# A gated-delta stage on one NeuronCore: recalled values through the chunk's inverse, decays by transposes, 512-wide outer products, another order at the first and last chunk

## What is computed

```python
L = where(strict, einsum(kb, ki) * decay, 0)          # kb = ki * beta
rhs = concat([vi * beta, kb * exp(gi)])
u, wk = split(triangular_solve(L + eye, rhs))
v_new = u - wk @ S
o = (qi * exp(gi)) @ S + attn @ v_new
S = S * exp(g_last) + (ki * exp(g_last - gi)).T @ v_new
```

## Time and profile before

| what | value |
|---|---|
| median of 3 runs | 1588.41 us (1588.24 to 1590.96) |
| the profiled execution's own time | 1588.98 us |
| its span, first to last instruction | 1587.2 us |
| PE / DVE / ACT / POOL busy share of the span | 93% / 57% / 41% / 13% |
| mean granted PE clock | 0.951 |

### The profile page before, as it was taken

One profiled execution on the slowest core, in us unless ns is written; L12 is line 12 of the kernel. 1 busy time (PEld: TensorE's weight loads), 2 busy tenths in 40 slices (PEclk: granted clock), 3 DMA queues, 4 the chain that ended last, 5 costly groups with the idle time before them and its releaser, 6 DMA issues. The chain is left out here.

```text
span 1587.2 us, 31920 instructions
## 1 busy us (share of the span) xinstructions
PE 1479.2 (93%) x13294; PEld 1320.5 (83%) x13294; DVE 900.5 (57%) x1197; ACT 648.6 (41%) x1108; POOL 208.7 (13%) x217
## 2 busy tenths in 40 slices
PE   6999989899889999999999998879879999999994
PEld 6999978889889999999999997458867777777773
DVE  5676534755465443444444754543366777676776
ACT  5343534442143222222232413552434565665661
POOL 0111024554011000000011100220011000000002
PEclk8999999999889999999999997889879999999997
DMA  6678240000352323231334530005137888888886
GB/s 177 226 267 280 78 120 2 2 2 3 107 156 72 106 79 106 79 103 57 91 91 131 151 103 21 1 1 134 72 121 240 287 289 294 290 295 268 272 284 239
DMA packets 169741, 226.13 MB, mean 142 GB/s; under 512 B 11272, under 2 KB 134689, under 8 KB 169545
## 3 DMA queue, kind: packets, MB, share of 16 engines
q1 hardware_dynamic: 160246, 191.44, 38.7%
q0 software_dynamic: 8512, 30.48, 5.3%
q10 hardware_dynamic: 862, 2.50, 0.4%
HBM read 188.78 MB, written 37.88 MB: 143 GB/s over the span
## 5 line engine op out<-in xcount | busy, mean ns | idle before, releaser
L276 DVE TENSOR_TENSOR w_lo<-w_raw,w_hi 128x2048 fp32r<-128x2048 f32 (+1 forms) x71 | 153.9, 2172 | 91.4 <-ACT w_hi L268 91.4
L268 ACT ACTIVATE w_hi<-w_raw 128x2048 fp32r<-128x2048 f32 (+1 forms) x71 | 128.1, 1810 | 124.0 <-PE P L221 118.5
L221 PE MATMUL P<-xf_hi,w_hi 128*128 128x260 f32 x704 | 141.8, 282 | 2.0 <-DVEq L1764 1.2
L221 PE MATMUL P<-xf_hi,w_lo 128*128 128x260 f32 x704 | 141.9, 283 | 0.0
L221 PE MATMUL P<-xf_lo,w_hi 128*128 128x260 f32 x704 | 141.7, 283 | 0.0
L221 PEld LDWEIGHTS P<-xf_hi,w_hi 128*128 128x128 f32 x704 | 108.5, 188 | 2.6 <-issue 1.4
L221 PEld LDWEIGHTS P<-xf_hi,w_lo 128*128 128x128 f32 x704 | 108.5, 188 | 0.0
L221 PEld LDWEIGHTS P<-xf_lo,w_hi 128*128 128x128 f32 x704 | 108.2, 188 | 0.0
L221 PE MATMUL P<-xa_hi,w_hi 128*128 128x260 f32 x512 | 104.1, 285 | 2.7 <-DVE xa_lo L319 2.7
L221 PE MATMUL P<-xa_hi,w_lo 128*128 128x260 f32 x512 | 104.1, 285 | 0.0
L221 PE MATMUL P<-xa_lo,w_hi 128*128 128x260 f32 x512 | 103.9, 285 | 0.0
(11 more groups left out here) (553 smaller groups left out, 3320.5 us busy)
## 6 DMA issues: line engine op xcount, KB each, us to landing
raw_more_moe<-in_moe_w_gu_dram SPq DMA_DIRECT2D x64, 512.0 KB, 5.3
w_raw<-in_moe_w_gu_dram SPq DMA_DIRECT2D x64, 512.0 KB, 5.4
w_raw<-in_dense_w_gu_dram SPq DMA_DIRECT2D x44, 512.0 KB, 4.5
expert_out<-zeros POOLq DMA_DIRECT2D x40, 512.0 KB, 4.1
w_raw<-in_a_w_in_dram SPq DMA_DIRECT2D x32, 512.0 KB, 5.0
raw_more_moe<-in_moe_w_down_dram SPq DMA_DIRECT2D x32, 512.0 KB, 4.8
w_raw<-in_moe_w_down_dram SPq DMA_DIRECT2D x32, 512.0 KB, 4.7
w_raw<-in_dense_w_down_dram SPq DMA_DIRECT2D x16, 384.0 KB, 4.0
```

The lines of the kernel that those rows point to most:

```text
L221: ins = nc.tensor.matmul(out[:, b], w, x[:, b * HALF:(b + 1) * HALF], start=(first and n == 0), stop=(last and n == 2))
L268: ins = nc.scalar.activation(hi, raw, ACT.Copy)
L276: ins = nc.vector.tensor_tensor(lo, raw, hi.bitcast(F32), ALU.subtract)
```

## The change

- **Recall.** POOL decays the keys in place (`decay_keys`), `recall` multiplies them with the state directly (before the inverse is joined), DVE subtracts the product from the values (`less_recalled`), and one `solve` puts the difference through the inverse. `weigh_F`, `solve_keys`, the negated copy and the exponentials `e_tok` go.
- **Decays** are spread by transposes of a broadcast column, not by matmuls.
- **Key norms.** `factors` on DVE adds epsilon to the sums itself, and no longer waits for ACT's square root.
- **Sample outer products** are 512 wide, 2 for each step and not 8: the deltas are masked (`mask_deltas`) and the keys kept (`k_keep`). They start at level 8 of the last chunk, where `sample_back` has moved ahead of `level_two`.
- **First chunk.** `values`, `query_sums` and the second chunk's `decay` move behind its level 2; the exponential table is loaded at the phase's start; three of six copies of edge rows go to DVE.
- **POOL** scales the diagonal blocks first and the corner blocks (`scale_corner`) after the pieces.
- **Last chunk.** Its output gathers in bank 1 (`last_from_state` before the solve); its squares are one ACT instruction for each group, summed by DVE; the prompt's last `add_state` on DVE stands behind the gate.
- **Weights of the output projection.** The first chunk's high part (ACT) and low part (POOL, `EarlyWeights`), four of eight high parts of the activations and the first low part are made at the end of the delta phase. For this the buffers lie otherwise: the inverse's own where the weight chunk will be.

The diff, cut to its core and with 8 columns of indentation less inside functions:

```diff
-        LTc, LT12, cc = big("LTc", g), big("LT12", g, n), small("c", g, n)
-        nc.gpsimd.tensor_tensor(LTc, LTc, per_head(cc, 64), ALU.mult)
-        prep[g].done(nc.gpsimd.tensor_tensor(LT12[upper], LT12[upper], per_head(cc[upper], 64), ALU.mult), "pool", n, "LT")
+        LTc = big("LTc", g)
+        prep[g].done(nc.gpsimd.tensor_tensor(LTc, LTc, per_head(small("c", g, n), 64), ALU.mult), "pool", n, "LT")
...
+    def scale_corner(g, n):
+        LT12 = big("LT12", g, n)
+        ins = nc.gpsimd.tensor_tensor(LT12[upper], LT12[upper], per_head(small("c", g, n)[upper], 64), ALU.mult)
...
+    def decay_keys(g, n):
+        prep[g].after(pool, n, pe="qk", act="e_row")
+        prep[g].done(nc.gpsimd.tensor_tensor(tokens(1, g, n), tokens(1, g, n), big("ER", g), ALU.mult), "pool", n, "k_dec")
...
-            chain[g].after(pool, n - 1, pe="Wk", pool="FE")
+            inv[g].after(pool, n - 1, pe="Y32")
...
-    def weigh_F(g, n):
...
+        nc.gpsimd.tensor_tensor(d_mask[:, k], prod[:, k].unsqueeze(1).broadcast_to([128, TS, 128]),
                                 cols(c, CPLACE, TS).unsqueeze(2).broadcast_to([128, TS, 128]), ALU.mult).then_inc(s_masked, 1)
...
+            if last and s in (2, 4):
+                mask_deltas(s // 4)
...
                 part(g, n + 1, 2)
+            for g in both:
+                scale_corner(g, n + 1)
+            for g in both:
+                decay_keys(g, n + 1)
+    early.low(pool, lambda eng: inv[1].after(eng, NCH - 1, pe="W64", act="F22"))
...
-            ins = pe.matmul(bank(g, 3)[:, h], G(g, n)[:, h:h + 1].broadcast_to([128, 128]), ident, start=True, stop=True)
+            ins = pe.transpose(bank(g, 3)[:, h], G(g, n)[:, h:h + 1].broadcast_to([128, 128]), ident)
...
+    def recall(g, n):
+        chain[g].after(pe, n - 1, dve="S")
+        chain[g].after(pe, n - 1, dve="x")
+        prep[g].after(pe, n, pool="k_dec")
+        chain[g].done(full(bank(g, 2), tokens(1, g, n), big("S", g, n)), "pe", n, "KS")
...
+    def solve(g, n):
...
-        chain[g].after(pe, n - 1, dve="x")
...
+        if n:
+            chain[g].after(pe, n, dve="VS")
...
+        ins = full(bank(g, 2), big("F", g), big("VP", g, n))
...
-    def solve_keys(g, n):
-        chain[g].after(pe, n, pool="FE")
-        chain[g].done(full(bank(g, 0), big("KS", g, n), big("FE", g)), "pe", n, "Wk")
...
+    def last_from_state(g, n):
...
+        for h in range(HL):
+            pe.matmul(bank(g, 1)[:, h], tokens(0, g, n)[:, h], big("S", g, n)[:, h], start=(h == 0), stop=False)
...
+    def last_from_chunk(g, n):
...
+            ins = pe.matmul(bank(g, 1)[:, h], big("AT", g, n)[:, h], big("VT", g)[:, h], start=False, stop=(h == HL - 1))
...
-        for r in range(4):
-            for j in range(2):
-                at = slice(32 * (2 * gp + j), 32 * (2 * gp + j) + 32)
-                ins = pe.matmul(c.P[:, 4 * j + 3, r * 128:(r + 1) * 128], k_mask[at, k, 4 * i + r], prod[at, k], start=True, stop=True)
+        for j in range(2):
+            at = slice(32 * (2 * gp + j), 32 * (2 * gp + j) + 32)
+            ins = pe.matmul(c.P[:, 4 * j + 3].rearrange("p (r v) -> p r v", r=4), k_keep[at, k], d_mask[at, k, 4 * i:4 * i + 4],
+                            start=True, stop=True)
...
-    for step in (keys, key_scores, query_scores, values, first, query_sums):
+    for step in (keys, key_scores, query_scores, first):
...
+            if last and s == 8:
+                sample_back()
+            if last and s >= 16:
+                sample_outer(1 if s == 16 else 3)
...
+            if s == 2 and not n:
+                for step in (query_sums, lambda g, _: decay(g, 1)):
+                    for g in both:
+                        step(g, 0)
+                sample_rows()
+            if last and s >= 8:
+                sample_outer({8: 0, 16: 2, 32: 4}[s])
...
+        if n:
+            for g in both:
+                recall(g, n)
...
             join_two(g, n)
...
             for g in both:
-                solve_keys(g, n)
+                last_from_state(g, n)
+            sample_outer(5)
+        for g in both:
...
-        exp(small("e_tok", g, n), G(g, n), prep[g], n, "e_tok")
...
+        copy(k_keep, k_row).then_inc(s_read, 1)
...
+    nc.scalar.activation(L.s_col[:, 0:1], cols(c, CEPS, 1), ACT.Exp)
...
+        for step in (corners, join, corner):
...
+    early.high(act, lambda eng: inv[0].after(eng, NCH - 1, act="F22", pe="W64"))
...
+    chain[0].after(act, NCH - 1, dve="x")
+    chain[1].after(act, NCH - 1, pe="KS")
+    split.high(nc, c, act, range(HL))
...
-        prep[g].after(dve, n, act="root")
-        rt, cc, c2 = small("ssk", g, n), small("c", g, n), small("c2", g, n)
-        own_chain.link(tt(cc, rt, rt, ALU.mult))
+        prep[g].after(dve, n, act="sq_k")
+        cc, c2 = small("c", g, n), small("c2", g, n)
+        own_chain.link(nc.vector.tensor_scalar(cc, small("ssk", g, n), EPS, None, ALU.add))
...
+    def less_recalled(g, n):
+        prep[g].after(dve, n, dve="VP")
+        chain[g].after(dve, n, pe="KS")
+        VP = big("VP", g, n)
+        chain[g].done(tt(VP, VP, bank(g, 2), ALU.subtract), "dve", n, "VS")
...
+    for part in range(3, 6):
+        dve.wait_ge(edge_turned, part + 1)
+        nc.vector.tensor_copy(edge_rows[:, part * 512:(part + 1) * 512], c.P[0:11, part - 3]).then_inc(edge_read, 1)
...
+            if last and s == 16:
+                sample_update(0)
+                sample_update(1)
+            if last and s == 32:
+                sample_update(3)
...
+            if s == 2 and not n:
+                for step in (queries, query_sums):
+                    for g in both:
+                        step(g, 0)
+                for g in both:
+                    left(g, 1)
...
+            if last and s == 16:
+                sample_update(2)
...
-                sample_update(0)
+                sample_update(4)
         if more:
-            for step in (query_scores, first, values, queries, query_sums):
+            for g in both:
+                query_scores(g, n + 1)
+        if n:
+            for g in both:
+                less_recalled(g, n)
+        if more:
+            for step in (first, values, queries):
                 for g in both:
                     step(g, n + 1)
...
-            for q in (1, 2, 3, 4):
-                sample_update(q)
...
-            new_values(g, n)
-    sample_update(5)
-    for g in both:
-        add_state(g, NCH - 1)
-    sample_update(6)
+            sample_update(5)
+        for step in (new_values, state_values):
+            for g in both:
+                step(g, n)
+        if more:
+            for g in both:
+                query_sums(g, n + 1)
     for g in both:
         sums_out(g, NCH - 1)
-    sample_update(7)
-    for step in (norm_out, gate_out):
+    sample_update(6)
+    for step in (norm_out, gate_out, add_state):
         for g in both:
             step(g, NCH - 1)
+    sample_update(7)
+    split.low(nc, c, dve, range(1))
...
+class EarlyWeights:
...
+    def high(self, act, free):
...
+        for i, part in enumerate(self.halves):
+            ins = nc.scalar.activation(c.w_hi[:, 0, part], c.w_raw[:, 0, part], ACT.Copy)
...
+    def low(self, pool, free):
...
+        for i, part in enumerate(self.halves):
...
+            ins = nc.gpsimd.tensor_tensor(c.w_lo[:, 0, part], c.w_raw[:, 0, part], c.w_hi[:, 0, part].bitcast(F32), ALU.subtract)
...
-    nc.scalar.activation(c.w_hi[parts[0]], c.w_raw[parts[0]], ACT.Copy).then_inc(hi_half, 1)
-    split.high(nc, c, act, range(0, 1))
-    nc.scalar.activation(c.w_hi[parts[1]], c.w_raw[parts[1]], ACT.Copy).then_inc(c.hi_done, 1)
-    split.high(nc, c, act, range(1, KT))
+    split.high(nc, c, act, range(HL, KT))
...
-    nc.vector.tensor_tensor(c.w_lo[parts[0]], c.w_raw[parts[0]], c.w_hi[parts[0]].bitcast(F32), ALU.subtract).then_inc(lo_half, 1)
-    split.low(nc, c, dve, range(0, 2))
-    dve.wait_ge(c.hi_done, st.base + 1)
-    nc.vector.tensor_tensor(c.w_lo[parts[1]], c.w_raw[parts[1]], c.w_hi[parts[1]].bitcast(F32), ALU.subtract).then_inc(c.lo_done, 1)
-    split.low(nc, c, dve, range(2, KT))
+    split.low(nc, c, dve, range(1, KT))
```

293 lines of the change are left out of this document (146 added, 147 removed).

## The result

The changed kernel takes 1580.62 us (median of 5 runs, 1578.15 to 1582.66) against 1588.8 of the kernel before (5 runs): ratio 0.9945, 95% interval 0.9934 to 0.9956, 8.2 us less. The forecast was 1566.5 with a range from 1559 to 1577: the sign was right, the gain about a third of the 22.3 forecast, and the time lies outside the range. The profiled execution took 1578.15 us, the shortest of the five, with a span of 1576.2, 11.0 less than before. So the profiles show where the time went, and medians and ratios what it is worth.

What follows compares the result with a forecast made beforehand. PE's issue order was taken to bound the delta phase. Gains of 6 (head), 3.5, 2 and 0.8 (boundaries) and 10 (last chunk) sum to 22.3 us off 1588.98, given as 1566.5, range 1559 to 1577.

Steps and rivals of the forecast that it cites:

- PE's stream is the phase's clock: Delta phase: PE's issue order sets its time, so what leaves PE's stream saves its time unless DVE comes last.
- Head, 6 us: Head and chunk 0: level 4 starts at 245.5 in place of 251.57, 6 us gained, ends 3.5 and 9.5.
- POOL against DVE: Chunk boundaries: POOL's run without a wait keeps DVE out, priced at 1 us each, 2.5 as the bad end.
- the three boundaries: Chunk boundaries: shorter or reordered PE rows gain 3.5, 2 and 0.8 us.
- The sign that I had named: Chunk boundaries: PE waiting over 2 us for DVE would show the theory wrong and point to DVE as the bound.
- rival 2: Last chunk, perhaps head: PE's clock at 0.50 gives back 8 us, 1574, or 1576 with both; chance 0.13.
- Rival 1: Chunk boundaries: DVE is the bound, PE's savings return as waits and the head loses 2; 1574 us, chance 0.17.
- Last chunk, 10 us: Level 8's second half to the projection: PE's rows and waits give 11.6 us less, taken as 10, ends 5 and 12.5.
- Rival 3: Last chunk: outer products without overlap and at slow clock hold up PE's in-order stream; slower than before, 1610 us, chance 0.03.
- Decays and early split: Decays' PE time halves by transposes; the projection weights' split lies beside some 10 us of PE's last-chunk rows.
- rival 5: Decays: a transpose of a broadcast column costs as a product, 4 x 1 us, 1570; chance 0.02.

Runs made afterwards that it cites:

- the combined kernel: Changed kernel with DVE's decayed queries behind state's values and query sums, POOL's decay_keys behind the level 4 piece, and sample-state fades moved: 1558.0 us, ratio 0.9807.

## Why the prediction was right and wrong

- **PE's stream is the phase's clock:** right as far as the stream goes. Its busy time fell by 13.7 us, and the combined kernel, where PE waits at most 0.75 us for another engine between the head's first pieces and the projection, gains 33 us of the phase: more than my 22.3, since the kernel before lost time to the same causes. One reading was wrong: I gave PE gaps of 0.2 to 0.6 us over the middle of the phase, and left out its waits of 1.62 us at 279.09 and 2.28 at 307.27. The second stands behind DVE steps of 3.79 us under two POOL steps of 3.76, so the trace of before already showed a second case of DVE kept out.
- **Head, 6 us:** measured 7.2. The size was right, in part by luck: level one started at 232.83 and not at 235.5, and from there to level 4 it took 11.3 us and not 10. One reason was wrong. The wait for the root counts (3 us), the order of `values` and `query_sums` doesn't.
- **POOL against DVE: the step that failed.** I put "1 us at each boundary, and 2.5 as the bad end". Measured were 7.8 us at the first (8.48 less 0.68) and 2.9 and 3.2 at the others. I had the row of 2.31 us over four POOL steps in hand, wrote that DVE may be kept out for a whole run, and then priced a run of ten by the row of 0.58. The bad end should have been the length of the run: some 7 us by my own sum, and more, as pieces, squares and a fade followed without a wait. I counted the run up to `decay_keys` only, and didn't look at what POOL could start next once DVE was early. By my forecast the three boundaries should give 6.3; they took 10.8. These 17.1 us and 0.4 lost in the levels of chunk 1, less the 5.0 that head and last chunk gave above the forecast, are the whole miss of 12.5 us. The sign that I had named, a wait of PE for DVE of over 2 us at a boundary, came with 8.19. The Trainium skill (page SBUF — State Buffer, section SBUF: two separate sides) says that the pair of ports is held by the one that starts first for the whole instruction, and that the other blocks. That DVE is blocked agrees with the trace. What I had concluded from it, that DVE waits for the one instruction under way, doesn't: eight POOL steps went by, and the measurement decides.
- **The clock behind the gaps:** rival 2 had the mechanism but for the most part the wrong place. No window of 0.50 lies in the last chunk, and the head has one at 0.66 (234 to 238). The windows of 0.50 lie behind the new waits at the boundaries, and before and within `sample_scores` (2.7 us with its first product, 2.04 for 1.12 and 8.97 for 7.17).
- **Rival 1** was nearest in kind. It named DVE at the boundaries, with the row of 2.31 us and POOL's longer run among its reasons, and gave 1574: too low, as it let the savings there come back and no more, and the boundaries lost 10.8 us on top. The number of DVE's steps is not the cause: the combined kernel has the same steps, and DVE is early enough.
- **Last chunk, 10 us:** measured 13.8. My sum gave 11.6, and I took 1.6 off for clock and small waits; the clock stayed at 1.00, so nothing was to be taken off. Above the sum lie 2.2 us: 1.9 from the outer product (1.06 us to the next row, not 1.3) and 0.6 from the waits (0.9 and not 1.5), less 0.3 for the tail (4.97 us behind PE's last transpose, not 4.7). The Trainium skill (page TensorE: Matmul & The Clock Gate, Part 3: Packing small matmuls — row/col tiling) says that products on different row groups run beside each other; my estimate by it was 8.4 us for the eight. The trace agrees, 8 x 1.06 = 8.5. Rival 3 is out.
- **Decays and early split:** right. Put back alone they cost 3.3 to 3.5 and 2.2 to 3.3 us; rival 5 is out.

## What to carry to other kernels

When an edit makes DVE early, look what POOL runs at the new time: a DVE step from two SBUF operands beside an unbroken row of POOL steps has the row's whole length as its bad end, not one step. Order such DVE steps behind everything that PE waits for, put long POOL work where DVE has none of them, and if neither can be done, let POOL wait for its own last step now and then. Gaps of 1.5 to 8 us on PE cost 1.3 to 3.2 more through the clock at four places here and nothing at two others (1.82 us in the changed kernel, 2.28 in the one before), so a gap's price is a range, and the first waits to remove are those ahead of long runs of products.

## What I had not expected of the hardware

- At a pause of 0.08 us between two POOL steps DVE came through, six times of six, and at seven seams in a row without one it did not. But some seams without a visible pause let it in too (266.39, 0.93 us in the changed kernel, and 270.24, 1.45 us in the kernel with one fade earlier). What decides at a seam stays open.
- The step is kept out even where it is small: DVE's two `SCALAR_TENSOR_TENSOR` of 128x4 took 3.79 us together beside two fades, at 300.37 in the changed kernel, and PE waited 2.26 for what is queued behind them. One of them takes 0.16 where POOL has nothing to do (423.75). The kernel before had the same wait (2.28).
- An f32 outer product step costs 1.06 to 1.09 us to the next row, as 2 x 512 columns or as 8 x 128.
